# A decoder step on one core: first tile, gates' products and attention scores in another order

## What is computed

```
z = rms_norm(x, norm1) @ w_in                      # 1024 -> 2312 columns, with 8 gate columns (i, f)
group A: mLSTM matrix memory, 4 heads, dk 64, dv 128, exact chunked form
group B: sliding-window attention, 8 query heads, 2 kv heads, head_dim 64, window 128,
         logits = q.k / 8 + rel_bias[bucket(distance)], softmax with one sink per head
x = x + concat(A, B) @ w_out
x = x + moe(rms_norm(x, norm2))                    # top 4 of 32 experts, clamped SwiGLU
y = rms_norm(x, final_norm)
```

## Time and profile before

| what | value |
|---|---|
| runs of the kernel before | 1519.29 us median of 3 (1518.84 to 1520.31) |
| the profiled execution | 1518.44 us |
| its span in the profile | 1516.7 us |
| PE busy | 1447.8 us (95%) |
| DVE, ACT, POOL busy | 1273.2, 1054.7, 180.5 us |
| mean granted clock of PE | 0.965 of 2.4 GHz |

### The profile page before, as it was taken

The page is one execution under the profiler, slowest core; times in us unless marked ns, Lnnn a source line. Parts: engine busy times, 40 slices in busy tenths (PEclk is TensorE's granted clock), DMA queues, the critical chain, the costliest instruction groups (busy, mean ns, idle before and its releaser), DMA issues.

```text
span 1516.7 us, 21417 instructions
## 1 busy us (share of the span) xinstructions
PE 1447.8 (95%) x7157; PEld 1062.5 (70%) x7157; DVE 1273.2 (84%) x1234; ACT 1054.7 (70%) x961; POOL 180.5 (12%) x186
## 2 busy tenths in 40 slices
PE   6999997878999999999999999999999999999993
PEld 5999865755777777777777777777777777777772
DVE  4344466369999999999999999999999999999995
ACT  4454443356787878777777878787878777777875
POOL 3000131142000001110000000000001110000000
PEclk9999997668999999999999999999999999999997
DMA  7311222149999999999999999999999999999994
GB/s 229 119 56 56 80 95 92 47 161 350 381 378 377 371 374 371 375 368 370 363 376 378 374 377 376 371 371 377 374 373 372 368 368 371 366 373 375 387 357 158
DMA packets 170596, 464.78 MB, mean 306 GB/s; under 512 B 14228, under 2 KB 28192, under 8 KB 170288
## 3 DMA queue, kind: packets, MB, share of 16 engines
q1 hardware_dynamic: 157240, 430.99, 76.4%
q0 software_dynamic: 8880, 24.00, 7.0%
q10 hardware_dynamic: 4440, 9.36, 1.8%
HBM read 447.90 MB, written 23.59 MB: 311 GB/s over the span
## 4 chain that ended last, share of the span: by engine, by line
PE 91%; DVE 4%; ACT 1%; issue 1%; ACTq 1%; DVEq 1%; DMA 1%; POOLq 0%; SPq 0%
PE ps L1738 87%; PE ps L1741 4%; DMA acc_rows<-reg_a,pass_tok 0%; ACT ring L1136 0%; DVE reg_w L1466 0%; DVE reg_z L1543 0%; DVE ring L1159 0%; DVE ring_r L1179 0%; DVE ring L1729 0%; DVE ring_r L1170 0%; DVE ring L1443 0%; DMA ring<-acc_rows 0%; DVE reg_b L1439 0%; DVE reg_b L1338 0%; DVE reg_z L1393 0%
## 5 line engine op out<-in xcount | busy, mean ns | idle before, releaser
L1738 PE MATMUL ps<-ring_r,reg_z_r 128*96 128x512 f32 x4608 | 1097.7, 395 | 0.0
L1738 PEld LDWEIGHTS ps<-ring_r,reg_z_r 128*96 128x96 f32 x4608 | 736.9, 162 | 308.9
L1063 ACT ACTIVATE ring_r<-ring 128x2048 fp32r<-128x2048 f32 x387 | 736.3, 1915 | 169.8 <-PE ps L1738 167.6
L451 DVE TENSOR_TENSOR ring_r<-ring,ring_r 128x2048 fp32r<-128x2048 f32 x355 | 797.7, 2284 | 51.2 <-ACT ring_r L1063 51.1
L730 POOL DMA_INDIRECT acc_rows<-reg_a,pass_tok x32 | 48.8, 1525 | 1004.5 <-ACT reg_a L1080 884.0
L1738 PE MATMUL ps<-reg_a_r,ring_r 128*128 128x264 f32 (+1 forms) x576 | 110.1, 286 | 0.0
L1738 PE MATMUL ps<-ring_r 128*128 128x256 f32 (+3 forms) x372 | 102.4, 324 | 0.0
L1738 PEld LDWEIGHTS ps<-reg_a_r,ring_r 128*128 128x128 f32 x576 | 90.6, 188 | 2.4 <-issue 2.2
L1086 ACT ACTIVATE reg_z_r<-ps 128x384 fp32r<-128x384 f32 x130 | 58.8, 479 | 37.8 <-PE ps L1741 37.8
L1666 DVE TENSOR_TENSOR ring_r<-ring,ring_r 128x1024 fp32r<-128x1024 f32 x64 | 77.7, 1213 | 0.0
L1738 PEld LDWEIGHTS ps<-ring_r 128*128 128x128 f32 (+1 forms) x372 | 68.0, 185 | 7.8 <-issue 0.5
(11 more groups left out here) (324 smaller groups left out, 951.2 us busy)
## 6 DMA issues: line engine op xcount, KB each, us to landing
ring<-in_w_gate SPq DMA_DIRECT2D x131, 1024.0 KB, 7.7
ring<-in_w_up SPq DMA_DIRECT2D x128, 1024.0 KB, 6.2
ring<-in_w_down SPq DMA_DIRECT2D x128, 1024.0 KB, 8.9
ring<-in_w_in SPq DMA_DIRECT2D x9, 1024.0 KB, 6.6
ring<-in_w_out SPq DMA_DIRECT2D x4, 1024.0 KB, 5.2
ring<-in_x_prompt SPq DMA_DIRECT2D x4, 512.0 KB, 8.6
reg_a<-in_x_prompt SPq DMA_DIRECT2D x4, 512.0 KB, 6.2
xhat_rows<-reg_w ACTq DMA_DIRECT2D x4, 512.0 KB, 2.7
```

The costliest lines, as they stand in the source:

```text
L451: return eng.tensor_tensor(rest_r(k), w, rounded_r(k).bitcast(F32), ALU.subtract)
L1063: act.activation(rounded_r(k), ring[:, slot_of(k), :], ACT.Copy).then_inc(hi_ready, 1)
L1738: return pe.matmul(out, lhsT, rhs, start=start, stop=stop, skip_group_check=True)
```

## The change

ACT keeps two of its eight first transfers; POOL issues the other six, right behind the identity and ahead of the slot table. ACT squares tile 2, and DVE normalises it, behind the first weight piece instead of ahead of tile 1's second half. On PE, step 0 (the gates, first half of the rows) stands behind tile 1's transposes and step 1 behind tile 3's. `att_scores` is called for even n only and makes the scores of pairs n and n + 1, in the order head x of pair n, head x of pair n + 1, for x = 0, 1; it waits for the logits of pair n - 1. Each pair still has its own increment of `s_psum`.

```diff
--- before.py
+++ after.py
@@ -587,6 +587,12 @@
             pool.drain()
             pool.affine_select(ident[:, :], ident[:, :], [[-1, P]], ALU.not_equal, 1.0, base=0,
                                channel_multiplier=1).then_inc(ident_made, 1)
+            pool.dma_start(relT, a["rel_bias"].rearrange("b h -> h b"), allow_slow_non_contiguous=True).then_inc(relT_in, 16)
+            pool.dma_start(b_if, a["b_if"].rearrange("a n -> n a"), allow_slow_non_contiguous=True).then_inc(consts_in, 16)
+            pool.dma_start(reg_w[0:8, 0:P], a["norm1"][0].rearrange("(c p) -> c p", p=P)).then_inc(consts_in, 16)
+            pool.dma_start(reg_w[8:16, 0:P], a["norm2"][0].rearrange("(c p) -> c p", p=P)).then_inc(consts_in, 16)
+            pool.dma_start(reg_w[16:20, 0:P], a["m_gain"][0].rearrange("(c p) -> c p", p=P)).then_inc(consts_in, 16)
+            pool.dma_start(sink_bc, a["sinks"].to_broadcast([P, AH])).then_inc(consts_in, 16)
             pool.memset(tab0[:, :, 1:2], 0.0)
             pool.iota(tab0[:, :, 0:1].bitcast(I32), [[0, NE], [0, 1]], base=TT, channel_multiplier=1)
             pool.drain()
@@ -752,13 +758,6 @@
 
             act.dma_start(n1_bc, a["norm1"].to_broadcast([P, D])).then_inc(n1_in, 16)
             act.dma_start(wif_v, w_in[:, :, GATE_COL:GATE_COL + 8]).then_inc(wif_in, 16)
-            act.dma_start(b_if, a["b_if"].rearrange("a n -> n a"), **slow).then_inc(consts_in, 16)
-            vec = reg_w[0:20, 0:P]
-            act.dma_start(vec[0:8, :], a["norm1"][0].rearrange("(c p) -> c p", p=P)).then_inc(consts_in, 16)
-            act.dma_start(reg_w[8:16, 0:P], a["norm2"][0].rearrange("(c p) -> c p", p=P)).then_inc(consts_in, 16)
-            act.dma_start(reg_w[16:20, 0:P], a["m_gain"][0].rearrange("(c p) -> c p", p=P)).then_inc(consts_in, 16)
-            act.dma_start(sink_bc, a["sinks"].to_broadcast([P, AH])).then_inc(consts_in, 16)
-            act.dma_start(relT, a["rel_bias"].rearrange("b h -> h b"), **slow).then_inc(relT_in, 16)
 
 
             def square(i):
@@ -788,11 +787,11 @@
             square(0)
             square(1)
             round_xT(0)
-            square(2)
             round_xT(1)
             act.wait_ge(wif_in, 16)
             act.activation(wif_r[:, 0], wif_v, ACT.Copy).then_inc(w_hi, 1)
             round_w_in(0)
+            square(2)
             square(3)
             round_xT(2)
             square(4)
@@ -1181,11 +1180,11 @@
             norm_rows(0)
             norm_rows(1)
             rest_of_xT(0)
-            norm_rows(2)
             rest_of_xT(1)
             dve.wait_ge(w_hi, 1)
             dve.tensor_tensor(wif_r[:, 1], wif_v, wif_r[:, 0].bitcast(F32), ALU.subtract).then_inc(w_lo, 1)
             rest_of_w_in(0)
+            norm_rows(2)
             norm_rows(3)
             rest_of_xT(2)
             norm_rows(4)
@@ -1855,19 +1854,22 @@
                 return last
 
             def att_scores(n):
-                i, c, lo = n // 4, n % 2, P if n < 4 else 0
+
+                i, lo = n // 4, P if n < 4 else 0
                 if n == 0:
                     pe.wait_ge(aksw_in, 32)
                     pe.wait_ge(*gtok_ready)
-                if n >= 2:
-                    pe.wait_ge(logit_ready, n - 1)
+                else:
+                    pe.wait_ge(logit_ready, n)
                 for x in range(2):
-                    h = head(n, x)
-                    rs, g = slice(c * HD, c * HD + HD), h // GRP
-                    keys = zT[rs, ZAK, 0:T] if g == c else ak_swap[rs, :]
-                    last = mm(ps[2 + c][:, 256 * x + lo:256 * x + 256], zT[rs, ZAQ + h // 2, i * P:(i + 1) * P],
-                              keys[:, (i - 1) * P + lo:(i + 1) * P])
-                last.then_inc(s_psum, 1)
+                    for c in range(2):
+                        h = head(n + c, x)
+                        rs, g = slice(c * HD, c * HD + HD), h // GRP
+                        keys = zT[rs, ZAK, 0:T] if g == c else ak_swap[rs, :]
+                        last = mm(ps[2 + c][:, 256 * x + lo:256 * x + 256], zT[rs, ZAQ + h // 2, i * P:(i + 1) * P],
+                                  keys[:, (i - 1) * P + lo:(i + 1) * P])
+                        if x:
+                            last.then_inc(s_psum, 1)
 
             def att_pT(n):
                 i, c = n // 4, n % 2
@@ -1911,9 +1913,8 @@
                     for c in range(4):
                         last = tr(ps[4 + 2 * (i % 2) + q][:, c * P:c * P + r], x_tile[i][0:r, (4 * q + c) * P:(4 * q + c + 1) * P], r)
                     last.then_inc(xT_psum, 1)
-                if i == 2:
-                    steps(0)
-                    steps(1)
+                if i in (1, 3):
+                    steps(i // 2)
             pe.wait_ge(consts_in, 16 * CONSTS)
             tr(ps[3][:, 0:20], reg_w[0:20, 0:P], 20).then_inc(gate_pe, 1)
 
@@ -1934,7 +1935,7 @@
                         last = tr(ps[3][:, 16 + i * 4:20 + i * 4], g_rows[3][0:4, ts], 4)
                     last.then_inc(gate_pe, 1)
                 n = m - FIRST_PAIR
-                if 0 <= n < PAIRS:
+                if 0 <= n < PAIRS and n % 2 == 0:
                     att_scores(n)
                 if 0 <= n - 1 < PAIRS:
                     att_pT(n - 1)
```

## The result

The change takes 1509.38 us (median of 4, 1508.62 to 1509.83) against 1519.55 (median of 4, 1518.84 to 1520.31): ratio 0.9937, 95% interval 0.9925 to 0.9948. That is 10.2 us less, more than the 7.4 forecast and just inside the range's lower end of 1509.0. The profiled execution took 1508.62, its span is 1506.9 instead of 1516.7.

What follows compares the result with a forecast made beforehand. PE was taken to bound the kernel from 27.67 us on, with waits before. The start's 1.2 and the scores' 6.2 sum to 7.4 us, from the median 1519.29 to 1511.9; range 1509.0 to 1517.0.

Steps and rivals of the forecast that it cites:

- What bounds the kernel: PE is busy throughout the projection from 27.67 to 160 us, so each PE microsecond saved there is one of the kernel.
- Scores, "certain" part: Attention scores: eight blocks instead of sixteen save eight times 0.30 us of entering and leaving the 64-row form, 2.4 us.
- Scores, overlap: Score blocks: passes on different halves run side by side, 8 passes in 5 slots; 3.8 us, 6.2 with the 2.4.
- at 128 columns the eight weight loads set the pace: Score blocks of 128 columns: eight weight loads take 0.88 us against 0.84 for the passes, so overlap saves nothing.
- The upper end, 8.3: Score blocks: most that two pairs at once could save, with four of eight passes hidden everywhere, 8.3 us.
- The Trainium skill's rule: Score blocks: tiles of the array on different rows work in parallel; with it 6.2 us, without it 2.4.
- The start: Before projection step 2: earlier first tiles and the new order let step 2 start at 26.45 instead of 27.67, 1.2 us.
- rival C: Passes overlap, but projection step 1 runs at the low clock and the start costs 1.1: 5.1 us gain, 1514.2; chance 0.13.
- Small loads on GpSimd: Six loads moved from ACT's to POOL's queue: table lands by 21 at worst, needed at 25.8, so cost 0.
- rival E: GpSimd's transfers run one after another, so ACT waits for the table at 45: 12 us slower, 1531; chance 0.04.
- Rival B: Score passes do not overlap, only blocks are merged: 3.6 us gain, 1515.7; chance 0.22.
- D: Score passes do not overlap and step 1 runs at the low clock: 1.3 us gain, 1518.0; chance 0.07.

Runs made afterwards that it cites:

- the scores alone: The kernel before with only the change's `att_scores` and its call for even n; 1508.91 us against 1517.79, ratio 0.994.
- Halves in a row: The changed kernel with a block's four products reordered so both products of one half follow each other; 1506.8 us against 1517.79 for the kernel before, ratio 0.9931.
- the start alone: The changed kernel with the old `att_scores`, one pair for each turn; 1516.45 us against 1518.27 for the kernel before, ratio 0.9989.
- the table first: The changed kernel with POOL's slot table made and written ahead of the six small loads; 1507.06 us against 1518.27 for the kernel before, ratio 0.9933.
- the change again: The changed kernel, unaltered, measured a second time; 1507.82 us against 1517.93 for the kernel before, ratio 0.9938.

## Why the prediction was right, and where it was wrong

- **What bounds the kernel**: right. From step 2 on PE had no gap, before and after, and the saving of the score blocks arrived whole: 8.73 in the stage and 8.9 in the time of the scores alone (7.1 to 11.2 by its interval).
- **Scores, "certain" part**: right. Eight blocks instead of sixteen; entering and leaving cost the 0.30 each that was worked out: (93.84 - 92.56) - 0.13 = 1.15, of which 4 x 0.21 = 0.84 are passes.
- **Scores, overlap: the step that failed.** "Passes start in order, and the second pass of a product uses the same rows as its first; so pass 2 of one runs beside pass 1 of the next, and 8 passes need 5 slots." It is 4 slots. Halves in a row shows that no such order holds between the halves. The same goes for "at 128 columns the eight weight loads set the pace": the change's blocks of 128 columns took four slots too, with the couples 0.11 apart behind the first. The records of PE's weight loads show couples as well, at 76.39 and 76.40 and at 76.50 and 76.51, so the loads of the two halves also run side by side. The upper end, 8.3, was the value; the stage gave 8.73. The 0.4 more fits the transposes behind a block, which take 0.49 for four (97.43 to 97.92) and 0.43 where none stands before (154.10 to 154.53). The change shows both in one kernel, 0.49 (93.84 to 94.33) and 0.44 (88.89 to 89.33). Blocks with transposes behind them are eight fewer, and eight times 0.06 are 0.5. No run isolates that term.
- **The Trainium skill's rule** ("TensorEngine Tiling (Array Packing)", "Key Properties": tiles on different rows work in parallel) is borne out by the couples at 0.01 us, for 64 rows with a bank each. My reading of an order on top of it is not.
- **The start: 1.2 forecast, 0.85 between the first two profiles, 0.3 to 3.0 in the time of the start alone.** The shifts of the first square (6.22 forecast, 6.11) and of the order were right; the assumption that tile 1 lands where it did was not: it came 0.6 late, which the table first takes back. "PE, done with step 0 by then or nearly" held, at 20.3. But the size of the gain is smaller than what the clock adds or takes: with neither part, with one, with both, and with both again, step 2 starts at 26.36, 27.78 or 27.31, 26.82 and 27.67. Step 1, which rival C had at the low level, ran at the high one in the change (24 starts in 2.81), while step 0 ran at the low one there, and the transposes of tiles 2 and 3 did in the change again. That is rival C seen too narrowly: I took the level of the earlier trace rows as belonging to a place in the kernel, where it moves about between executions, in the kernel before as well.
- **Small loads on GpSimd**: cost 0 on ACT's path, right, and the drain does wait for its transfers, which I had left open. The six landed at 9.65 and the table at 17.1, not the 14 and 21 of the bound. On ACT's queue `relT` took 11.8 us from its issue until POOL could copy from it, on POOL's queue 6.5 us to land. The slower rival E fell with them: they ran beside one another. That "I leave tile 0's landing as it was" held for tile 0 and not for tile 1.
- **Rival B** (no overlap) and **D** fell by the couples.
- **Range**: 1509.0 to 1517.0 held 1509.38 barely. The upper end of the overlap, 8.3 with a start of 1.2, gives 1509.8 and lay just inside; the further 0.4 of the transposes was in no term. That 1509.38 lies inside is partly luck: the same kernel took 1507.82 later, beside 1517.93 for the kernel before, a gain of 10.1 us. The sum of 7.4 was 2.8 short, of which 2.5 are the overlap and the transposes.

## What to carry to other kernels

The passes of products over 64 rows cost half when the two halves of the partitions are both at work in one block with a bank each. Their order within the block is free, so group them by what is simplest. Each entry into that form costs 0.30 us, so put several products behind one; more than four were not tried. Work that PE does without a gap is where a saving arrives whole. At a start that waits for transfers, count which tile lands second: the first tile's square moved by 1.2 us, the second's only by 0.2, and step 0 follows the second. And where the clock changes levels, a single profile does not price a gain below 3 us: the middle stage and the start of one kernel moved by 2.2 and 0.85 between two executions.

## What the runs showed of the hardware

- Two products on rows 0 to 63 and 64 to 127 with separate banks start within 0.01 us of each other (92.78 and 92.78, 93.09 and 93.10), even when another of the first one's half stands between them in the program (93.05 and 93.06).
- POOL's drain ends only after the transfers that POOL issued have landed: 17.32 behind a landing at 17.1, 11.82 behind one at 11.3, and the first drain's successor moved from 10.58 to 2.60 when it had none to wait for.
- The granted clock of PE's stretches before 28 us and between 155 and 371 us differs between executions of one kernel, at the same work: step 0 in 2.70 or 4.88 us from first to last start, the middle stage in 214.2 or 216.4.
- What remains open: why tile 1 lands later with the loads on POOL's queue at 2 to 5 us (no run shows which of the six does it, or how), and whether two halves that write to one bank would still overlap, which was not tried.
